# Four edits at once in a 256-token transformer block in float32: start order, relative-bias table, modulation fold, residual rows

## The reference, cut to what matters

```
h = rmsnorm(x, g[0]);  proj = h @ w_in
bias = table[t5_bucket(q_pos - key_pos)]          # 8 heads, depends on the distance alone
logits = q @ k * HEAD_DIM**-0.5 + bias            # sparse attention, first block
mixed = sum(gates * up) @ w_out
x = x + rmsnorm(mixed, g[1])                      # the residual rows
h = rmsnorm(x, g[2]);  m = square(relu(h @ w_up)) @ w_down;  x = x + rmsnorm(m, g[3])
shift, scale, gate = split(silu(c) @ w_ada + b_ada)   # modulation vectors of the second block
```

## Time and profile before

| What | Value |
|---|---|
| Median of three runs | 2230.3 us (2230.04 to 2232.3) |
| The profiled execution: its time | 2230.79 us |
| its span, first to last instruction | 2229.0 us |
| PE busy, weight loads busy | 99%, 93% |
| DVE busy, ACT busy, POOL busy | 67%, 48%, 3% |
| DMA | 473.74 MB, 213 GB/s |
| Longest wait of PE for another engine after the start | 0.9 us |

### The profile page before, as it was taken

One profiled execution on the slowest core, in us unless ns is written; L12 is line 12 of the kernel. 1 busy time (PEld: TensorE's weight loads), 2 busy tenths in 40 slices (PEclk: granted clock), 3 DMA queues, 4 the chain that ended last, 5 costly groups with the idle time before them and its releaser, 6 DMA issues.

```text
span 2229.0 us, 37697 instructions
## 1 busy us (share of the span) xinstructions
PE 2205.0 (99%) x15998; PEld 2064.1 (93%) x15998; DVE 1496.9 (67%) x1878; ACT 1069.1 (48%) x1418; POOL 60.7 (3%) x65
## 2 busy tenths in 40 slices
PE   7999999999999999999999999999999999999998
PEld 7999999999999888988988988998889989999986
DVE  6788588888889757554555555555756555688655
ACT  5444445544444546444443443444656555444443
POOL 1000000000000001000000000000100000011000
PEclk9999999999999999999999999999999999999999
DMA  8866676777777765656656656656664445788763
GB/s 257 249 191 183 196 237 217 236 251 256 261 245 261 269 210 167 200 193 194 195 192 196 191 196 199 198 186 208 234 199 141 135 141 163 260 294 296 251 214 139
DMA packets 246273, 473.74 MB, mean 213 GB/s; under 512 B 21054, under 2 KB 25528, under 8 KB 244440
## 3 DMA queue, kind: packets, MB, share of 16 engines
q1 hardware_dynamic: 242888, 454.40, 63.7%
q0 software_dynamic: 3216, 16.92, 2.3%
HBM read 467.05 MB, written 4.21 MB: 211 GB/s over the span
## 4 chain that ended last, share of the span: by engine, by line
PE 93%; DVE 3%; DMA 1%; issue 1%; ACT 1%; POOL 0%; POOLq 0%; SPq 0%; ACTq 0%; DVEq 0%
PE ps L852 19%; PE ps L853 19%; PE ps L854 19%; PE ps L845 10%; PE ps L847 10%; PE ps L846 10%; PE ps L780 1%; DVE tmp L1234 1%; PE ps L674 1%; DMA raw<-in_w_out 1%; DVE wloW L1206 1%; ACT whiW L884 1%; PE ps L769 0%; PE ps L760 0%; PE ps L759 0%
## 5 line engine op out<-in xcount | busy, mean ns | idle before, releaser
L852 PE MATMUL ps<-op0h,whiW 128*128 128x256 f32 x3376 | 942.0, 279 | 1.3 <-DVE wloW L1206 1.3
L854 PE MATMUL ps<-op0h,wloW 128*128 128x256 f32 x3376 | 933.3, 276 | 0.0
L853 PE MATMUL ps<-op0l,whiW 128*128 128x256 f32 x3376 | 933.2, 276 | 0.0
L1206 DVE TENSOR_TENSOR wloW<-raw,whiW 128x1024 fp32r<-128x1024 f32 (+1 forms) x504 | 611.0, 1222 | 338.1 <-ACT whiW L884 335.9
L884 ACT ACTIVATE whiW<-raw 128x1024 fp32r<-128x1024 f32 (+1 forms) x504 | 529.5, 1058 | 587.5 <-PE ps L854 452.5
L852 PEld LDWEIGHTS ps<-op0h,whiW 128*128 128x128 f32 x3376 | 634.7, 188 | 7.2 <-issue 5.6
L853 PEld LDWEIGHTS ps<-op0l,whiW 128*128 128x128 f32 x3376 | 634.8, 188 | 2.0 <-issue 1.4
L854 PEld LDWEIGHTS ps<-op0h,wloW 128*128 128x128 f32 x3376 | 634.7, 188 | 0.0
L1206 DVE TENSOR_TENSOR wloT<-raw,whiT 128x1024 fp32r<-128x1024 f32 (+1 forms) x264 | 316.4, 1208 | 274.3 <-ACT whiT L884 273.9
L884 ACT ACTIVATE whiT<-raw 128x1024 fp32r<-128x1024 f32 (+1 forms) x264 | 273.6, 1046 | 293.9 <-PE ps L847 249.5
L845 PE MATMUL ps<-whiT,op1h 128*128 128x512 f32 x640 | 249.5, 390 | 0.1
(11 more groups left out here) (269 smaller groups left out, 2015.7 us busy)
## 6 DMA issues: line engine op xcount, KB each, us to landing
raw<-in_w_in SPq DMA_DIRECT2D x256, 512.0 KB, 4.4
raw<-in_w_up SPq DMA_DIRECT2D x128, 512.0 KB, 3.9
raw<-in_w_down SPq DMA_DIRECT2D x128, 512.0 KB, 4.1
raw<-in_w_ada SPq DMA_DIRECT2D x96, 512.0 KB, 4.8
raw<-in_w_gate SPq DMA_DIRECT2D x96, 512.0 KB, 5.1
raw<-in_w_out SPq DMA_DIRECT2D x64, 512.0 KB, 4.5
raw<-in_w_branch SPq DMA_DIRECT2D x48, 512.0 KB, 5.0
raw<-in_w_proj_a SPq DMA_DIRECT2D x24, 512.0 KB, 5.3
```

The source lines that it names most:

```text
L852: pe.matmul(o, wh, xh[:, ka, :], start=first and m % 2 == 0, stop=False, skip_group_check=True)
L853: pe.matmul(o, wh, xl[:, ka, :], start=False, stop=False, skip_group_check=True)
L854: mm = pe.matmul(o, wl, xh[:, ka, :], start=False, stop=last, skip_group_check=True)
L1206: v.tensor_tensor(wlo[job.mode][q % NSPL][:, :, 0:job.n], x, h.bitcast(F32), ALU.subtract).then_inc(s_lo, 1)
```

## The change

1. At the start PE transposes the gain vectors first, DVE copies them (`vat`) before it scales the second tile of x, ACT and DVE do `high(i)` and `low(i)` ahead of `turn_x(i)`, and DVE scales the last two quarters of the second tile behind `turn_x(1)`.
2. The bias row is written to device memory in the order in which it is needed. One DMA copies each head's row 128 times within device memory, each time 513 numbers further on, so that a second DMA with a step of 512 reads the shifted rows directly into `bt`. The reversing matmuls, the ACT copies and the load of `flip` are gone.
3. `ada_fold` and `ada_columns` stand one chunk later.
4. The two residual tiles are added in a part `x1_add` of its own, one ahead of `low(291)` and one ahead of `low(292)`, in place of both at the end of `ep_wo`.

```diff
+SKEW = 128 * 513 + 384
-        for i in range(4):
-            q = of["pool1"].end + 11 + 2 * i
-            side(pe_at, q, "bias_flip", i)
-            side(act_at, q + 1, "bias_flip", i)
...
-        side(pe_at, ada_at[63] + 1, "ada_fold")
-        side(dve_at, ada_at[63] + 2, "ada_columns")
+        side(pe_at, ada_at[63] + 2, "ada_fold")
+        side(dve_at, ada_at[63] + 3, "ada_columns")
...
+            side(dve_at, of["wo3"].end + tt, "x1_add", tt)
             q = of["wo3"].end + 1 + tt
             side(act_at, q, "x1_square", tt)
...
-            pool.dma_start(scratch_e, erow[0:8, :]).then_inc(s_erow_w, 16)
-            pool.dma_start(flip[:, :], a["k_flip"]).then_inc(s_flip, 16)
+            pool.dma_start(bass.AP(scratch_e.tensor, 8 * SKEW, [[384, 8], [1, 384]]), erow[0:8, :]).then_inc(s_erow_w, 16)
+            pool.wait_ge(s_pe, of["pool1"].first)
             pool.wait_ge(s_erow_w, 16)
-            for i in range(4):
...
-                pool.dma_start(tmp[4 + i % 2][:, :].rearrange("p (h s) -> p h s", h=2),
-                               bass.AP(scratch_e.tensor, 768 * i, [[1, 128], [384, 2], [1, 256]])).then_inc(s_bt_in[i % 2], 16)
+            pool.dma_start(bass.AP(scratch_e.tensor, 0, [[SKEW, 8], [513, 128], [1, 384]]),
+                           bass.AP(scratch_e.tensor, 8 * SKEW, [[384, 8], [0, 128], [1, 384]])).then_inc(s_skew, 16)
+            pool.wait_ge(s_skew, 16)
+            pool.wait_ge(s_pwm, 4)
+            pool.dma_start(bt[:, :, :], bass.AP(scratch_e.tensor, 127, [[512, 128], [SKEW, 8], [1, 256]])).then_inc(s_bt, 16)
...
+            def x1_add(tt):
+                if tt == 0:
+                    v.wait_ge(s_xr, 16)
+                v.wait_ge(s_rstd, norm_no["mixed", tt])
+                v.scalar_tensor_tensor(X[:, tt, :], macc[:, tt, :], norm_col("mixed", tt)[1], X[:, tt, :], ALU.mult, ALU.add).then_inc(s_x1, 1)
```

More of the change, by code:

```diff
@@ L688, in pool_weight @@
                 mm.then_inc(s_pwm, 1)
[L690 to L695, removed]
-                pe.wait_ge(s_bt_in[i % 2], 16 * (i // 2 + 1))
-                pe.matmul(bank[4 + i % 2][:, :], flip[:, :], tmp[4 + i % 2][:, :], start=True, stop=True).then_inc(s_btp, 1)
             def scores1(h):
@@ L703, in scores1 @@
                     pe.wait_ge(s_pair[of["q1"].pair], of["q1"].after)
[L704 to L706 removed]
+                    pe.wait_ge(s_idxr, 12)
+                if h >= 2:
                     pe.wait_ge(s_ya, h - 1)
@@ L940, in pool_scale @@
                 act.activation(op1h[:, 2 * g:2 * g + 2, :], half(tmp[5]), ACT.Copy).then_inc(s_phi, 1)
-            def bias_flip(i):
-                act.wait_ge(s_btp, i + 1)
-                act.activation(bt[:, 2 * i:2 * i + 2, :], half(bank[4 + i % 2]), ACT.Copy).then_inc(s_bt, 1)
             def softmax1_exp(h):
@@ L1370, in softmax1_max @@
                     v.wait_ge(s_chi, 4)
-                if h < 2:
-                    v.wait_ge(s_bt, 4)
-                else:
+                    v.wait_ge(s_bt, 16)
+                    v.wait_ge(s_pwm, 4)
+                if h >= 2:
                     v.wait_ge(s_tr1, h - 1)
@@ L1560, in ep_wo @@
                         variance("mixed", tt, D)
-                    v.wait_ge(s_xr, 16)
-                    for tt in range(2):
-                        v.wait_ge(s_rstd, norm_no["mixed", tt])
-                        v.scalar_tensor_tensor(X[:, tt, :], macc[:, tt, :], norm_col("mixed", tt)[1], X[:, tt, :], ALU.mult, ALU.add).then_inc(s_x1, 1)
             def ep_up(job, b0, b1):
@@ L1700, in _, with norm_second @@
             row_var(0, 1)
+            v.wait_ge(s_vst, 1)
+            v.tensor_copy(vat[:, :], bank[7][:, 0:112]).then_inc(s_vat, 1)
             v.wait_ge(s_rstd, 2)
-            for i in range(4):
+            def norm_second(i):
                 x = x0[:, 1, 512 * i:512 * i + 512]
                 v.tensor_scalar(x, x, norm_col("x0", 1)[1], None, ALU.mult).then_inc(s_x0n, 1)
-                if i == 1:
-                    v.wait_ge(s_vst, 1)
-                    v.tensor_copy(vat[:, :], bank[7][:, 0:112]).then_inc(s_vat, 1)
-            for i in range(3):
-                turn_x(i)
-                low(i)
+            norm_second(0)
+            norm_second(1)
+            for i in range(3):
+                low(i)
+                turn_x(i)
+                if i == 1:
+                    norm_second(2)
+                    norm_second(3)
             for q in range(NQ):
```

33 lines of the change are left out of this document (11 added, 22 removed).

## The result

The changed kernel has a median of 2223.86 us (2222.78 to 2226.82, nine runs) against 2230.04 us (2228.7 to 2232.3, nine runs) for the kernel before. The ratio is 0.9975, 95% interval 0.9966 to 0.9984: faster by 0.25%. The forecast was 2225.2 us. In microseconds the interval is a gain of 3.6 to 7.6, with 6.2 between the medians.

A forecast was written before the change was run, and what follows sets the result against it. PE bounds the kernel, busy 2205.0 of 2229.0 us. The start 1.5, bias table 3.43, fold 0.78 and residual rows -0.65 sum to 5.06 us off the median 2230.3, giving 2225.2 us, range 2223.0 to 2227.6.

The forecast's parts named there:

- The start: Kernel beginning: first weight matmul at 15.22 in place of 16.73, gaining 1.5 us, between 0.8 and 3.1 by the clock's rise.
- the transposes count: Rival, start: clock's rise counted from PE's transposes, so the start gives 3.1 us, total 2223.6; chance 0.12.
- at a fixed moment: Rival, start: the clock's rise stays at 20.71, so the start gives 0.8 us, total 2225.9; chance 0.18.
- The bias table: Chunks 58 to 67: four reversing matmuls leave PE's list, gaining 3.43 us.
- The narrow margin at chunk 67: DVE's `low(67)` would be ready 0.2 us before PE asks; if missed, the bias table gains 3.0 us.
- The fold: At `ada_fold`: one chunk later, PE's wait goes and the fold's own 0.43 us remains, gaining 0.78 us.
- The residual rows: Behind `wo3`: wait at chunk 291 goes, new waits at chunk 292 and the transposes before 293; net loss 0.65 us.
- POOL was held: Rival, residual rows: POOL's 1/rms slowed beside DVE at both tiles, loss 1.2 us, total 2225.8; chance 0.08.
- The copy in device memory: Bias rows' 1,536 KB copy: 6.2 us, or 12.4 if reading and writing add up; sign: lands within 13 us.
- The slower rival: Copy starves weight loads, 0.44 us per us; PE waits past 19 us, slower past 30; chance 0.09, 0.04 slower.
- The sum: Whole kernel: 1.5 + 3.43 + 0.78 - 0.65 = 5.06 us gained.
- the main case: Whole kernel: all four terms as forecast, 2225.2 us, own range 2224.2 to 2226.2; chance 0.45.

The follow-up runs named there:

- a_warm: Changed kernel plus extra PE matmuls on a cleared tile no output uses, 12 ahead of the gains' transpose and 3 behind; 2228.04 us median.
- b_x1: Kernel before with only the residual rows added in two parts; 2231.21 us median, ratio 1.0005.
- a_nox1: Changed kernel with both residual additions put back in the epilogue of the last output projection; 2223.98 us median.
- a_turn: Changed kernel with the second residual addition ahead of the row waiting for ACT's squares, and PE's transposes of these rows one chunk later; 2221.43 us median.
- a_: Prefix for kernels that are the changed kernel with a change of its own; medians from 2221.43 to 2228.45 us.
- b_: Prefix for the kernel before with one edit alone: start order 2228.02, bias table 2225.98, later fold 2229.28, split residual rows 2231.21 us.
- a_wo1: Changed kernel with only the 2048 KB load of x held until the first output projection `wo1` is done; 2224.23 us median.
- a_late: Changed kernel with the 2048 KB load of x held until `wo1` is done and the second X load until POOL's ninth modulation sum; 2228.45 us.
- a_warm2: Changed kernel plus extra PE matmuls no output uses, 4 ahead of the gains' transpose and 2 behind; 2222.89 us median.

## Why the prediction was right, point by point

- **The start** (forecast 1.5, bounds 0.8 and 3.1). Sixteen transposes in a row, then the weights: right. They began at 11.52 and not 11.80, which is chance (11.62 to 11.81 in the four traces of the old order, 11.52 to 11.87 in the seven of the new one), and the first weight matmul followed the start of the last one by 0.07 us and not by a full step, so 14.84 and not 15.22. In the profiled pair chunk 1 starts 2.56 us earlier. Over all traces it starts at 20.7 in the mean of the four of the old order and at 18.9 in the seven of the new one without extra matmuls, so 1.8, a rough figure, since chunk 1 moves by 2.0 us within the first group and 1.2 within the second. Where the fast step had come by the second weight matmul, chunk 1 starts at 19.8 in two traces of the old order and at 18.3 in three of the new one: 1.5, the gain of the work alone. The forecast had that part right; that the clock added only a few tenths to it in the mean was luck. I took the fast step to keep its distance of 3.9 to 4.1 us from the first weight matmul, but one and the same start had it from 2.0 us ahead of it to 4.0 behind. The rival "the transposes count" was dismissed too easily: in four traces of the two orders the fast step came before the first weight matmul, 3.0 to 3.2 us after PE had begun on x, so work on transposes alone had sufficed there; in six others it came 5.8 to 8.9 us after. What decides between these stays open. The Trainium skill, page "TensorE: Matmul & The Clock Gate", Part 1, which I had weighed, says that the moment is not tied to a kernel's start and can differ from run to run; the traces agree, with moments from 14.63 to 20.71 us for the old order. Nor is the step at a fixed moment in all of them, as the rival had it: PE's early work in `a_warm` brought it to 7.5 us.
- **The bias table** (3.43): 3.52 in every pair, out of PE's list. The narrow margin at chunk 67 was 0.40 us and held.
- **The fold** (0.78): 0.80 in every pair.
- **The residual rows** (-0.65): -0.69. The old wait of 1.01 went, the new one at chunk 292 measured 0.5 (from 841.54 to 842.28 where a step is 0.23), that at the transposes 1.4. POOL was held beside the second addition, 2.59 us in place of 0.55, at the first tile alone, where nothing waited. `b_x1` and `a_nox1` show the loss by itself, put in and taken out; `a_turn` undoes both waits by two moves, the order of the parts and the later transposes.
- **The copy in device memory**: 13.2 us, just over the 6.2 to 12.4 between which I had set it, and over the 13 given as a sign. (The store of 8.3 us behind that range is issued at 1573 us, not where the copy falls.) The slower rival's price of 0.44 us for each us was too high, since even 61 us of copying made PE wait for nothing. Why the weight loads held up so well was not taken apart.
- **The sum** (5.06). The mean start and the three fixed terms give 1.8 + 3.52 + 0.80 - 0.69 = 5.4; the medians differ by 6.2. The forecast was 1.3 us high: 2223.86 lies in the stated range, but under the 2224.2 to 2226.2 that the main case had claimed for itself. The interval of 3.6 to 7.6 us holds 5.1, 5.4 and 6.2 alike, so what is left over need not be anything. In the profiled pair the table accounts for the whole: 2.56 + 3.52 + 0.80 - 0.68 from the four edits, -1.29, -1.18 and +0.21 at 266, 663 and 690, together 3.9, and the spans differ by 4.0. What the sum left out are the places where weight loads run beside other transfers. At chunks 267 and 664 the traced execution of after lost 2.5 us against before, but six of the eight other `a_` traces lose nothing at 267 and all eight nothing at 664, while before and the four `b_` kernels lose 0.3 to 0.8 at chunk 267. That accounts for the profiled execution being the slowest, and may account for a few tenths of the rest. Why these five meet the wait more often stays open.

## What to carry to other kernels

Before splitting a long operation into parts, write down what the second part now stands behind: here it came to stand behind a wait for ACT, which cost more than the old wait. Ask of the consumer too: the split paid once the second part stood one place higher and PE's transposes were asked for one chunk later. Where the engine that bounds the kernel runs an unbroken list, compare stretches of it between traces, chunk by chunk: terms of 0.7 us are exact there and lost in the medians. And a large transfer that is moved can cost nothing (`a_wo1`) or over 4 us (`a_late`, where it fell among weight loads that were needed soon and the wait was followed by a slow stretch of the clock).

## What the hardware showed that I had not expected

- The clock's step to 2.4 GHz fell at 14.63, 14.98, 19.86 and 20.71 us in four traces with the same order of the start, in which PE began on x at 11.6 to 11.8, and at 14.84, 14.97, 15.25, 17.32, 17.37, 17.59 and 17.67 us in seven of the new one, in which it began at 11.5 to 11.9. This moved chunk 1 by up to 2.0 us in the old order and 1.2 in the new, as much as the edit itself.
- In `a_warm2` PE's step was the fast one directly behind a pause of 2.18 us (four records in 1.90 us from 9.30 on), and stayed so. In `a_late`, 1.4 us after a wait of 2.23 us, the granted clock fell to 0.50, from 2008.14 to 2011.55. What tells the two cases apart is not shown.
- A copy of 1,536 KB within device memory, in rows of 1.5 KB, took 13.2 us beside the weight loads, and 15.2 in the median of four.
- POOL's operation on 128x1 took 0.55 us by itself, 1.46 beside a `low` of DVE and 2.59 beside a DVE addition that reads two tiles of 128x2048.
